# Prompt attention: at each pair's first tile, TensorE issues the values product ahead of the scores of three tiles later

## What is computed

```python
# forgetting heads (fox)
sc = einsum("bqhd,bkhd->bhqk", q, k) * scale
sc = sc + cum[query] - cum[key]                 # running sums of log forget gates
sc = where(k_pos <= q_pos, sc, -inf)
o = einsum("bhqk,bkhd->bqhd", softmax(sc), v)
# dilated heads: the same with a position bias, three (window, dilation) branches
# merged by their softmax denominators; here one bias table holds them all
```

## Time and profile before

| | |
|---|---|
| median of 3 runs | 1701.33 us (1699.52 to 1702.0) |
| the profiled execution | 1705.38 us, its span 1703.8 us |
| busy over the span | PE 95%, PEld 86%, DVE 80%, ACT 46%, POOL 34% |
| prompt attention | about 192 to 282 us of the span |
| its 32 steps, pairs 1 to 7 | 10.5 us a pair with masks, 9.9 us without |
| attention of the new positions | about 282 to 326 us |

### The profile page before, as it was taken

The page is one execution under the profiler, slowest core; times in us unless marked ns, Lnnn a source line. Parts: engine busy times, 40 slices in busy tenths (PEclk is TensorE's granted clock), DMA queues, the critical chain, the costliest instruction groups (busy, mean ns, idle before and its releaser), DMA issues.

```text
span 1703.8 us, 27739 instructions
## 1 busy us (share of the span) xinstructions
PE 1623.8 (95%) x9666; PEld 1461.8 (86%) x9666; DVE 1360.3 (80%) x3159; ACT 776.4 (46%) x1262; POOL 579.9 (34%) x513
## 2 busy tenths in 40 slices
PE   5999987797999999989999999999999999999997
PEld 4999744497999999989999999997888888888886
DVE  4224585354899999979999999997999999999996
ACT  4222374223434433367767777763333333333334
POOL 0000380002544534654334334433343333433320
PEclk9999997997999999999999999999999999999999
DMA  3342562712333423499999999999999999999991
GB/s 119 106 156 94 164 198 98 271 73 78 130 131 109 135 100 107 158 354 371 388 369 397 382 370 388 404 404 389 404 403 399 404 405 399 404 403 399 404 365 53
DMA packets 158620, 463.52 MB, mean 272 GB/s; under 512 B 18224, under 2 KB 64432, under 8 KB 154546
## 3 DMA queue, kind: packets, MB, share of 16 engines
q1 hardware_dynamic: 98930, 248.59, 39.7%
q0 software_dynamic: 50944, 178.96, 27.5%
q10 hardware_dynamic: 8640, 34.61, 5.0%
HBM read 406.12 MB, written 57.63 MB: 272 GB/s over the span
## 4 chain that ended last, share of the span: by engine, by line
PE 47%; DVE 21%; DMA 3%; issue 3%; ACT 1%; POOL 1%; another core or an unknown queue 0%; SPq 0%; DVEq 0%; ACTq 0%; POOLq 0%
PE va L230 10%; PE va L231 10%; PE va L232 10%; PE hp L230 4%; PE hp L231 4%; PE hp L232 4%; DVE gathered L1396 3%; DVE og L1901 3%; DVE ulo L1912 2%; PE ggp L1841 2%; DVE vw L1396 2%; DMA hidden_values<-gelu_out 1%; DVE sc L1606 1%; DVE oh L1900 1%; DVE X L1605 1%
## 5 line engine op out<-in xcount | busy, mean ns | idle before, releaser
L230 PE MATMUL hp<-mid_hi,uhi 128*128 128x384 f32 x1024 | 354.6, 346 | 9.1 <-issue 3.5
L231 PE MATMUL hp<-mid_lo,uhi 128*128 128x384 f32 x1024 | 345.2, 337 | 0.0
L232 PE MATMUL hp<-mid_hi,ulo 128*128 128x384 f32 x1024 | 343.8, 336 | 0.0
L230 PE MATMUL va<-vhi,ahi 128*128 128x512 f32 x768 | 299.7, 390 | 3.4 <-DVE hid L1396 2.7
L231 PE MATMUL va<-vlo,ahi 128*128 128x512 f32 x768 | 299.5, 390 | 0.0
L232 PE MATMUL va<-vhi,alo 128*128 128x512 f32 x768 | 299.4, 390 | 0.0
L1771 POOL DMA_INDIRECT gathered<-in_v_experts,eidx x160 | 175.0, 1094 | 311.6 <-DVE acc L2221 222.8
L1309 POOL TENSOR_TENSOR ulo<-uw,uhi 128x1024 fp32r<-128x1024 f32 x49 | 124.1, 2533 | 261.0 <-ACT uhi L1305 261.0
L230 PEld LDWEIGHTS hp<-mid_hi,uhi 128*128 128x128 f32 x1024 | 193.2, 189 | 14.5 <-issue 5.6
L232 PEld LDWEIGHTS hp<-mid_hi,ulo 128*128 128x128 f32 x1024 | 193.3, 189 | 0.0
L231 PEld LDWEIGHTS hp<-mid_lo,uhi 128*128 128x128 f32 x1024 | 193.1, 189 | 0.0
(11 more groups left out here) (314 smaller groups left out, 3413.1 us busy)
## 6 DMA issues: line engine op xcount, KB each, us to landing
uw<-in_u_experts SPq DMA_DIRECT2D x128, 512.0 KB
vw<-in_v_experts SPq DMA_DIRECT2D x68, 512.0 KB
more_v<-in_v_experts SPq DMA_DIRECT2D x60, 512.0 KB
gate_matrix<-gst ACTq DMA_DIRECT2D x12, 2048.0 KB
hidden_values<-gelu_out SPq DMA_DIRECT2D x72, 192.0 KB
hd_mid<-hidden_values SPq DMA_DIRECT2D x8, 1536.0 KB
gt_mid<-gate_matrix SPq DMA_DIRECT2D x8, 1536.0 KB
hd_freed<-hidden_values SPq DMA_DIRECT2D x7, 1536.0 KB
```

The costliest lines, as they stand in the source:

```text
L230: nc.tensor.matmul(out, a_hi, b_hi, start=first, stop=False)
L231: nc.tensor.matmul(out, a_hi, b_lo, start=False, stop=False)
L232: return nc.tensor.matmul(out, a_lo, b_hi, start=False, stop=last)
```

## The change

In PE's program two calls change places. Nothing else is touched, no instruction is added or taken away, and the queues of DVE, ACT, POOL and SP stand as they were.

```diff
                 for s in range(STEPS):
                     turn(s)
+                    if s and s % QB == 0:
+                        values(s // QB - 1)
                     if s + 3 < STEPS:
                         scores(s + 3)
-                    if s and s % QB == 0:
-                        values(s // QB - 1)
                 values(PAIRS - 1)
```

## The result

| | before | changed |
|---|---|---|
| median, 18 runs each | 1701.72 us | 1705.13 us |
| lowest and highest | 1699.52 and 1704.9 | 1702.24 and 1709.54 |
| ratio | | 1.0016 (95% interval 1.0008 to 1.0023) |

The change makes the kernel slower by 0.16%, 2.7 us (1.4 to 3.9); the two medians alone lie 3.4 us apart. Timed twice more against the kernel before, it came out at 1.0006 (0.9996 to 1.0016) and 1.0008 (0.9998 to 1.0018). The mean of the three is about 0.1%, 1.7 us. The profiled execution took 1709.54 us, its span 1708.0 us; it is the slowest of the 18 runs.

The account below looks back on a forecast made before the run. The attention's pairs were taken as bound by a PE-ACT-PE chain with DVE close behind; 1.60 + 0.71 + 0.64 + 0.16 + 0.11 + 0.11 = 3.3 us on 1701.33 gave 1704.6 us, range 1701.5 to 1708.5.

Parts of the forecast that it names:

- only ACT: Rival: in the attention's pairs only the delay by way of ACT counts, 0.9 us, 1702.2 us, no change; chance 0.14.
- Values earlier gain nothing: At tile 0 of a pair, values start 1.06 us sooner (1.50 with masks), copies come sooner, but this gains nothing.
- Scores later: Scores put behind the values make DVE's next maxima start 1.07 us later without masks, 0.97 us with them.
- ACT's path: Later `turn(4j+2)` delays ACT's copy of tile 2 by 0.11 us, 0.16 with masks; sets pairs 1, 5 and 7.
- DVE's path in pairs 3, 4 and 6: Late scores delay DVE's queue, less the slack before its reciprocal: 0.80, 0.71 and 0.64 us.
- the tie itself: In pairs with L840 (0.68 us), DVE's scaling ends level with PE's next first turn: 245.23 against 245.34 in pair 4.
- DVE's path in pair 2: Masks, L840 and no room on DVE: 0.97 us delay less 0.17 us slack costs 0.80 us.
- The seams: PE's unseen loss between values and scores in the new order: -0.1 to +0.1 us in each of seven places.
- The clock: Rival: TensorE's half-clock fall near the attention's end shifts, 1.8 us less or more: 1702.8 or 1706.4 us; chance 0.14.
- A microsecond in the attention moves the end by one: Work behind the attention hangs on its result without slack, so a microsecond lost or won there moves the end equally.
- The signs: Expected in the changed profile: freed value waits, seven new score waits of 1.7 to 2 us, later work shifted 3 us.

Follow-up runs that it names:

- r_after: The changed kernel timed again without any edit against the kernel before, for a second profile; measured 1.0006 (0.9996 to 1.0016).

## Why the prediction was right, and where not

- *Sign and place.* Slower, inside the range (1701.5 to 1708.5), at 1705.13 for a forecast of 1704.6. Both numbers carry luck: the set of before had risen by 0.4 us, and the later timings put the cost at 1.0 and 1.4 us. What holds is the mechanism with 1.95 us. That is nearer to the "only ACT" rival's 0.9 than to my own 3.3, and in the 0.2% that I had called no change. It also lies below the forecast's own range of 2.3 to 4.6 us, which was added up wrongly besides: 3.3 with -0.7 to +0.7 for the seams is 2.6 to 4.0. So the middle was set too high, and the first timing hid it.
- *Values earlier gain nothing.* Right. `turn(4j+1)` didn't move, the copies waited for less, nothing came sooner. The test with only the first values ahead says so too, where the copies waited less still and the pairs grew by a seam.
- *Scores later.* Right to 0.01 us in pair 6 (3.80 behind the turn) and to 0.03 in pair 5 (253.47, 3.83 behind the turn at 249.64).
- *ACT's path,* 0.11 to 0.16 us. Right: 0.12, 0.12 and 0.13 us in pairs 1, 5 and 7, though the scores were 1 us late there. In pair 5 ACT's copy of tile 2 starts 2.83 us behind its copy of tile 1 (253.90, 256.73), for 2.73 before. Only about half of these 0.1 us goes with `turn(22)`, 0.61 us behind which the copy starts (256.12), where I had 0.56. The other half had come already by L877 (2.21 us for 2.16), a lateness of ACT's own queue that I had put at nothing; what makes it isn't shown.
- *DVE's path in pairs 3, 4 and 6.* The mechanism is right, shown in pairs 4 and 6 by taking L840 away; its size was 0.80, 0.71 and 0.64 and is 0.50, 0.51 and 0.45. The term that was off is the tie itself. I took `turn(20)` to start when the scaling was through; in rows 3 and 8 it ended 0.11 us before (245.23, 245.34), and in the changed pair 6 it ends 0.06 before (269.87, 269.93), so 0.05 was room. The reciprocal comes 6.64 us behind the first turn in pair 6 changed; pair 5 of before has 6.06, 0.58 later and not 0.64. And from there to the scaling's end it is 3.61 us, where pair 4 of before took 3.69. There DVE's L835 began at 242.60, just behind the end of ACT's L877 at 242.57, whose result it reads, and 0.06 us later than it follows the scaling in the changed pair 6, where L877 is long through; that this was a wait is read from these times alone. 0.58 - 0.08 - 0.05 = 0.45.
- *DVE's path in pair 2.* Wrong, 0.80 for 0.12. This is the step that failed: I carried the tie of pair 4 over to pair 2 because both have L840, and gave DVE "no room" there and 0.17 us of slack. Pair 2 has masks, PE works longer, and DVE has more room. The first profile hid it. DVE's scaling and PE's turn at the end of pair 2, in the first profile of before:

```profile
224.42 0.68 DVE L830 TENSOR_SCALAR E<-E,rden 128x128 f32<-128x128 f32 x2
...
225.16 0.44 PE L773 MATMUL TE<-ident,E 128*128 128x128 f32 x2
```

  And in the second:

```profile
224.97 0.48 DVE L830 TENSOR_SCALAR E<-E,rden 128x128 f32<-128x128 f32 x2
...
225.83 0.38 PE L773 MATMUL TE<-ident,E 128*128 128x128 f32 x2
```

  The scaling took 0.68 us in the first, and ended at 225.10, hard before the turn. In the second it took 0.48, ended at 225.45, and 0.38 us lay between it and the turn. The slack before the reciprocal was hidden in the same way: other scalings were slow too in the first profile (128x384 in 1.00 us, 0.75 in the second), and the reciprocal came 0.58 us behind the maxima, 0.83 in the second (220.93, 221.76), which is 0.42 of slack and not 0.17. The pair takes 10.54 and 10.53 us all the same: the turn waited for PE. In `r_after` the scaling ends at 227.91 and the turn starts at 228.01, so the delay just used the room up. A near tie in one profile isn't yet a bound. What made the scalings slow in the first profile stays open.
- *The seams,* -0.7 to +0.7 us. In the changed order they cost nothing to be seen (3.70 and 3.70 us); one group more costs 0.16 us.
- *The clock.* The rival named the right size, 1.8 us at the last values, and this happened three times in three, but it isn't what decides: low stretches of 1.4 to 1.7 us come and go in both kernels. Of the 4.2 us by which the span of the first profiled execution grew, 2.7 lie between the first turn and the scan (96.1 against 98.8), the change's 1.95 us and the clock's ups and downs together, and 1.8 behind the scan, while the first turn came 0.2 sooner.
- *A microsecond in the attention moves the end by one.* Not shown. Behind the attention the profiles differ by up to 4 us of their own, as the last section tells.
- *The signs.* As forecast were DVE's freed wait, its new waits of about 2 us, the 1.67 us before `turn(26)` and the 0.1 us of pair 5. ACT's wait fell to 1.0 us a pair, not to 0.6 to 0.8. `turn(8)` to `turn(12)` is 0.12 us longer and not 0.8, and pair 2 loses no more than pairs 1 and 5, which I had named as a sign of being wrong.

## What to carry to other kernels

When a wait is freed by reordering an engine's queue, ask first whether the waiting engine's next step gets any sooner, and then who reads what was put behind. A block of work on the path isn't made cheaper by another order within it; it is made cheaper by moving the parts that nobody needs yet into a later wait of the same engine, at the price of a seam for each cut (0.16 us here). And read a tie from more than one pair and more than one profile before giving it a price.

## What the runs showed of the hardware

The largest scatter lies behind the attention. From ACT's first `qT` op (413.6 us in the kernel before) to its first `x2p` op (670.6) the profiles take either 257.0 or 253.3 us, whatever the kernel: 257.0 in the first two of before and the first of the changed kernel, 253.3 in the third of before and in the other two of the changed one. In this stretch DVE and POOL seem to stop one another. First the times of two DVE ops in the kernel before (minimum/median/maximum ns, first and last start):

```profile
L1637 DVE TENSOR_SCALAR ab<-ab x8: 201/279/2286, 452.1 to 706.2; 128x80 uint32<-128x80 uint32 x8
...
L1650 DVE TENSOR_TENSOR eq<-eq,XF x16: 944/960/3159, 457.2 to 712.4; 128x1280 bf16<-128x1280 bf16 x16
```

A place on its timeline:

```profile
597.18 2.39 POOL L1309 TENSOR_TENSOR ulo<-uw,uhi 128x1024 fp32r<-128x1024 f32 x1 [1.75 <-ACT uhi L1305]
...
597.35 2.29 DVE L1637 TENSOR_SCALAR ab<-ab 128x80 uint32<-128x80 uint32 x1
```

And one on that of `r_after`:

```profile
600.57 1.49 DVE L1646 TENSOR_TENSOR eq<-ranks,rank 128x2560 bf16<-128x2560 bf16 x1
...
600.81 3.51 POOL L1309 TENSOR_TENSOR ulo<-uw,uhi 128x1024 fp32r<-128x1024 f32 x1 [1.75 <-ACT uhi L1305]
...
602.21 3.80 DVE L1650 TENSOR_TENSOR eq<-eq,XF 128x1280 bf16<-128x1280 bf16 x2
```

An op of 0.28 us took 2.29 where it began 0.17 us behind a POOL op of 2.39 us; both ended at about 599.6. In `r_after` POOL's op met DVE the other way round: it began 0.24 us behind DVE's L1646 and took 3.51 us, and the two DVE ops of 0.96 that followed took 3.80. The Trainium skill ("SBUF — State Buffer", SBUF: two separate sides) says that DVE and GpSimd share a port pair as an exclusive lock: of a GpSimd op and a DVE op with two SBUF inputs or in a 2-port mode, the one that starts first holds it for the whole instruction and the other blocks. These rows agree with it, with L1646 and L1650 as ops with two inputs; that L1637, with one, runs in such a mode no row shows.

The 3.7 us arise at one place. Before the op L1513 that begins at 617.6 us in the kernel before, ACT waits 8.5 us for DVE's chain in the three profiles of 257.0 us, and 4.6 or 4.7 us in the three of 253.3. In the 30 us ahead of it DVE's ops L1619, L1637, L1658 and the two of L1650 took 2.40, 2.29, 2.37 and 1.83 us in the first three, and 0.19, 0.7, 0.23 and 3.8 in the other three, each within 0.03 us. The differences come to 2.2 + 1.6 + 2.1 - 2.0 = 3.9 us. So which of DVE's ops are long makes the two lengths of the stretch. That POOL makes them long, and that a shift of a few tenths of a microsecond decides which, fits the rows shown; it is argued and not proven, since no run took an op of POOL away.

The granted clock was low at nearly the same place of pair 0 (about 199 to 204 us) in five of the six profiles of the two kernels, with PE's program the same up to there, and not in the sixth. So it isn't bound to the program alone, nor quite free of it.
